# Fifty-six transposes of the identity on TensorE around the first tile of x in a hybrid decoder layer

## What is computed

```python
h = rms_norm(x, norm_w[l])
proj = jnp.einsum("btd,dc->btc", h, w_in[l])
gdn_qkv, gdn_z, gdn_b, gdn_a, moba_qkv, moba_z, gates = jnp.split(proj, SPLIT_POINTS, axis=-1)
...
merged = jax.nn.sigmoid(g_gdn) * y_gdn + jax.nn.sigmoid(g_moba) * y_moba
x = x + jnp.einsum("btd,de->bte", merged, w_o[l])
```

## Time and profile before

| | us |
|---|---|
| median of 3 runs | 1585.48 |
| lowest and highest run | 1585.01, 1586.07 |
| span of the profiled execution | 1583.4 |
| TensorE busy in it | 1559.0 |
| VectorE busy in it | 1084.3 |
| ScalarE busy in it | 797.1 |

### The profile page before, as it was taken

One profiled execution on the slowest core, in us unless ns is written; L12 is line 12 of the kernel. 1 busy time (PEld: TensorE's weight loads), 2 busy tenths in 40 slices (PEclk: granted clock), 3 DMA queues, 4 the chain that ended last, 5 costly groups with the idle time before them and its releaser, 6 DMA issues.

```text
span 1583.4 us, 20787 instructions
## 1 busy us (share of the span) xinstructions
PE 1559.0 (98%) x7767; PEld 1299.2 (82%) x7767; DVE 1084.3 (68%) x1331; ACT 797.1 (50%) x1063; POOL 191.0 (12%) x181
## 2 busy tenths in 40 slices
PE   6999999999999999999999999999999999999999
PEld 6888888888888888888888888888888887887787
DVE  6655655745646646656558778867676999978864
ACT  5434534444445445445445347556565765555542
POOL 4202001002002001011011011010101111102020
PEclk9999999999999999999999999999999999999999
DMA  8314315224234224233234338667557777878783
GB/s 270 90 32 126 81 34 149 56 62 123 54 86 115 70 57 121 60 81 98 60 86 118 119 135 252 209 171 254 131 188 191 234 234 238 231 225 176 224 183 57
DMA packets 198048, 217.04 MB, mean 137 GB/s; under 512 B 7843, under 2 KB 140198, under 8 KB 196902
## 3 DMA queue, kind: packets, MB, share of 16 engines
q1 hardware_dynamic: 177030, 162.73, 34.0%
q0 software_dynamic: 20960, 53.52, 14.7%
HBM read 191.03 MB, written 29.39 MB: 139 GB/s over the span
## 4 chain that ended last, share of the span: by engine, by line
PE 92%; DVE 3%; issue 2%; ACT 1%; DMA 1%; SPq 0%; DVEq 0%; ACTq 0%
PE bank L823 15%; PE bank L827 15%; PE bank L825 14%; PE bank L1273 11%; PE bank L1275 11%; PE bank L1277 11%; PE bank L852 2%; PE bank L928 2%; PE bank L946 1%; DVE ring_lo L2282 1%; PE bank L1023 1%; PE bank L931 1%; PE bank L857 1%; PE bank L873 1%; PE bank L874 1%
## 5 line engine op out<-in xcount | busy, mean ns | idle before, releaser
L823 PE MATMUL bank<-h_hi_r,w_hi 128*128 128x512 f32 x1008 | 408.2, 405 | 0.0
L827 PE MATMUL bank<-h_hi_r,w_raw_r 128*128 128x512 f32 x1008 | 395.0, 392 | 0.0
L825 PE MATMUL bank<-h_lo_r,w_hi 128*128 128x512 f32 x1008 | 393.4, 390 | 0.0
L2282 DVE TENSOR_TENSOR ring_lo<-operands,ring_hi 128x1024 fp32r<-128x1024 f32 x224 | 271.5, 1221 | 112.6 <-ACT ring_hi L1646 111.9
L1646 ACT ACTIVATE ring_hi<-operands 128x1024 fp32r<-128x1024 f32 x224 | 235.4, 1060 | 214.2 <-PE bank L1277 161.9
L827 PEld LDWEIGHTS bank<-h_hi_r,w_raw_r 128*128 128x128 f32 x1008 | 189.1, 188 | 41.8
L823 PEld LDWEIGHTS bank<-h_hi_r,w_hi 128*128 128x128 f32 x1008 | 189.7, 188 | 35.6
L825 PEld LDWEIGHTS bank<-h_lo_r,w_hi 128*128 128x128 f32 x1008 | 189.9, 188 | 34.7
L1273 PE MATMUL bank<-ring_hi,h_hi_r 128*128 128x512 f32 x480 | 190.2, 396 | 1.3 <-issue 1.3
L1275 PE MATMUL bank<-ring_lo,h_hi_r 128*128 128x512 f32 x480 | 188.6, 393 | 0.0
L1803 DVE TENSOR_TENSOR w_raw_r<-w_raw,w_hi 128x2048 fp32r<-128x2048 f32 x64 | 151.4, 2365 | 37.2 <-ACT w_hi L1333 36.0
(11 more groups left out here) (333 smaller groups left out, 2183.1 us busy)
## 6 DMA issues: line engine op xcount, KB each, us to landing
w_raw<-in_w_in_dram SPq DMA_DIRECT2D x64, 1024.0 KB, 6.0
operands<-in_w_in_dram SPq DMA_DIRECT2D x64, 512.0 KB, 4.6
operands<-in_w_o_dram SPq DMA_DIRECT2D x32, 512.0 KB, 5.2
operands<-in_w_in_dram POOLq DMA_DIRECT2D x16, 512.0 KB, 8.2
gates<-e_block POOLq DMA_DIRECT2D x16, 512.0 KB, 5.7
operands<-in_w_out_gdn_dram SPq DMA_DIRECT2D x16, 512.0 KB, 5.0
operands<-gates SPq DMA_DIRECT2D x16, 512.0 KB, 7.0
operands<-in_w_out_moba_dram SPq DMA_DIRECT2D x16, 512.0 KB, 5.4
```

The lines of the kernel that those rows point to most:

```text
L823: pe.matmul(PJ[slot % 2][:], w_hi[slot % 2][:, c], h_hi[:, k, :], start=(k == 0), stop=False, skip_group_check=True)
L825: pe.matmul(PJ[slot % 2][:], w_hi[slot % 2][:, c], h_lo[:, k, :], start=False, stop=False, skip_group_check=True)
L827: mm = pe.matmul(PJ[slot % 2][:], w_lo[slot][:, c], h_hi[:, k, :], start=False, stop=(k == KT - 1), skip_group_check=True)
L2282: dve.tensor_tensor(ring_lo[:, n % RINGS, :], operand(q, p, j), ring_hi[:, n % RINGS, :].bitcast(F32), ALU.subtract).then_inc(s["op_lo"], 1)
```

## The change

A helper `ready(n)` issues n transposes of `ident` by `ident` into bank A1. Forty-eight stand ahead of `x_turn(0)`, and eight between `x_turn(0)` and `x_turn(1)`. They count no semaphore. The lines behind move down by seven.

```diff
+            def ready(n):
+
+                for i in range(n):
+                    pe.transpose(A1[:, tile4(i % NT)], ident[:], ident[:])
+
+            ready(48)
             x_turn(0)
+            ready(8)
             x_turn(1)
             x_turn(2)
```

## The result

| | before | after |
|---|---|---|
| median of 21 runs, us | 1586.07 | 1588.55 |
| lowest to highest | 1584.57 to 1587.85 | 1587.42 to 1592.94 |
| span of the profiled execution | 1583.4 | 1585.9 |

The ratio is 1.0017, with a 95% interval of 1.0012 to 1.0023. The change made the kernel 2.5 us slower by the medians, 2.7 by the ratio (0.0017 x 1586). The forecast was 1585.1, the range ended at 1587.8. Of the 3.4 us between forecast and median, 0.6 lie in the kernel before, whose median over 21 runs is 1586.07 and was 1585.48 over the three known then.

What follows compares the result with a forecast made beforehand. It took TensorE, busy 98% of the span and slow-clocked until about 26.2 us, as the bound. Span 1583.4 - 0.4 = 1583.0, plus 2.08 around it, gave 1585.1 us; range 1584.0 to 1587.8.

Steps and rivals of the forecast that it cites:

- The transposes were free: Start, ahead of tile 0: the 48 fit TensorE's 8.2 us of cover if the clock rises within 6.0 us; no cost.
- ScalarE's fourth copy of hi(1): Tile 1 at the start: no longer waiting for TensorE, it starts at 19.79 instead of 20.33, gaining ScalarE 0.54 us.
- scale(3) began right behind the lo part of `w16`: VectorE, tile 3: scale(3) follows at 23.38 at once, so VectorE can use only 0.34 us of ScalarE's gain.
- VectorE decided when the products start: First-weight products: VectorE's lo part holds them, so nearly all of TensorE's 2.4 us gain turns into waiting.
- The gain of the start: First-weight products start at 30.29 instead of 30.68 us, a gain of 0.39 us.
- VectorE's work moving up: VectorE's lo part of the first weights ends at 30.15 instead of 30.49 us, 0.34 us earlier.
- the release: First-weight products: TensorE starts 0.14 us behind VectorE's end, where the kernel before showed 0.19.
- 2.08 us around the span: Whole kernel: time outside the profiled span, added to the predicted span of 1583.0 to give 1585.1 us.
- The new wait of 1.9 us ahead of the products: TensorE before the first-weight products: finished at 28.4 us, it idles 1.9 us for VectorE.
- rival 2: Start: clock rises, then falls in a gap, so tile 2 starts slow as now; 1585.4 us, chance 13%.
- Rival 1: Start: transposes do not lift the clock, so tile 0 is 2.1 us late; 1587.1 us, chance 32%.
- the last term of the costs: Fetching the extra instructions, not priced apart by the trace: taken as zero, with 0.3 us either way in the range.

Runs made afterwards that it cites:

- loop2: Second run of the changed kernel with its 48 and 8 transposes issued from two hardware loops of four each; ratio 0.9995.
- loop: Changed kernel with its 48 and 8 transposes issued from two hardware loops of four each; median 1585.67 us, ratio 0.9999 against the kernel before.
- gb: Kernel before, with the late gate load that VectorE awaits issued ahead of two operand loads instead of behind them; ratio 0.9996.
- b5: Kernel before plus 5 very small matmuls (10 pairs of weight load and matmul) ahead of tile 0; ratio 1.0000.
- b12_2: Second run of the kernel before plus 12 very small matmuls (24 pairs of weight load and matmul); ratio 0.9999.

## Why the prediction was wrong

**What held.** The transposes were free: I had the rise 5.1 us behind the first and the end at 10.7; the profile has the rise between 4.3 and 5.7 and the end at 10.9. ScalarE's fourth copy of hi(1) ran unpaced, and scale(3) began right behind the lo part of `w16`. VectorE decided when the products start: they come at 30.11, 0.05 us behind the end of L1810 and 0.23 behind the last transpose, whose pace is 0.11.

**The gain of the start came by another way.** I had 0.34 us for VectorE's work moving up and 0.05 for the release, 0.39 in all, and it was 0.57. But L1810 (L1803 before) begins at 27.78 instead of 27.85, which is 0.07 earlier, and the whole load of x came 0.09 earlier in this profile. Scale(3) did start 0.50 earlier and then took 2.25 us instead of 1.82, while GpSimd's part beside it took 1.56 instead of 3.18. Of the changed kernel, and the last row of before:

```profile
23.22 2.25 DVE L2187 SCALAR_TENSOR_TENSOR x_tiles<-x_tiles,mgt,norm_w_rows 128x1536 f32<-128x1536 f32 x1
...
23.16 1.56 POOL L681 TENSOR_SCALAR x_tiles<-x_tiles,mgt 128x512 f32<-128x512 f32 x1 [0.15 <-ACT mgt L1584]
```
```profile
23.78 3.18 POOL L681 TENSOR_SCALAR x_tiles<-x_tiles,mgt 128x512 f32<-128x512 f32 x1 [0.68 <-ACT mgt L1577]
```

The other 0.50 us are L1810 itself, 2.28 instead of 2.64 (GpSimd was through with tile 3 ahead of it this time, at 26.6 instead of 28.3; that this is the reason is not shown), and 0.14 of the release. On the release the prediction misread the rows: in the kernel before the last transpose of tile 3 started at 30.65 and the products at 30.68, so TensorE's own work came last and not VectorE, which had ended at 30.49. That the total lies near the forecast is in part luck. The sum also put 2.08 us around the span; in the changed kernel's profiled run it is 1.6 (1587.49 and 1585.9), so some 0.5 of it was that a median stood beside another execution.

**What did not come.** The new wait of 1.9 us ahead of the products: tile 2 and the beginning of `beta_alpha(0)` ran at the slow pace, so TensorE was through just when VectorE was. That is rival 2 in its first half, and loop2 shows that it doesn't happen in every execution. It cost nothing, since VectorE decides: loop, with the fall, has its products at 30.08, loop2 without it at 30.15.

**Rival 1 falls, though the time lay on its side.** Transposes of the identity alone took TensorE to the fast pace (the level of 2.4 GHz) within 6 us. The rule of the Trainium skill, "TensorE: Matmul & The Clock Gate", Part 4: PE-mode transpose, that the full clock does not engage for them, is not what this chip does with these transposes in float32; the measurement decides. By its time, 1587.1, that rival would have looked half right; its mechanism was not there. The Trainium skill's account of falls between bursts, in the same page's section on HAM oscillation, agrees with the trace of the changed kernel in that a fall came, 0.50 behind thin work and a gap of 1.65 us; in loop2 the same gap brought none.

**The step that failed** is the last term of the costs: "The extra instructions have to be fetched, which the trace does not price apart; I take zero, with 0.3 us either way in the range." In the trace it was worth up to 3.0 us, from 0.57 ahead to 2.5 behind, of which the load of the gate has some 2.2 and the load of 1436 us has 0.6. By the medians the changed kernel lies 2.0 to 2.5 us above before and the two loop kernels 0.3 to 0.5 below, so the added length is worth 2.3 to 2.9. I had looked for the price of the fetch at the place of the instructions. It was paid in the straight-line code behind the loop, by two loads on other queues that had no slack. The rows to see this were in the trace of before: single instruction packets in the list of queues, and a wait of VectorE of 1.2 us for the gates on the last-ending chain. Neither says in which direction a shift would go, but the range should have reached to the landing of that load a few microseconds later.

The start's gain is also less the change's own than it looks. The kernel gb has the start of before unchanged, and its tile 2 ran at the fast pace by itself:

```profile
20.95 1.76 PE L1203 MATMUL bank<-ident,x_tiles 128*128 128x128 f32 x12 [0.76 <-DVE h_lo_r L2188]
```

Its products started at 30.44. In two other kernels without any transpose, with a few very small matmuls at the start, they came at 30.17 (b5) and 30.10 (b12_2), as early as in the changed kernel. The moment of the rise differs from one execution to the next, and how much of the 0.57 us belongs to the change is not shown: 0.33 against gb, nothing against these two.

## What to carry to other kernels

An instruction added at the start of an unrolled program moves every later block of instructions that is fetched, and a block that falls on a load without slack can cost more than the instruction. Before believing a small gain or loss, run the same length without the work, and the same work in a hardware loop. When a time moves and the edited place does not explain it, match the traces instruction by instruction and look where the distance changes. A load that the chain waits for belongs ahead of loads that can be late; here that took most of the sensitivity away, and the next load with a waiting engine kept its own.

## What the runs showed of the hardware

- TensorE's instructions come in packets of 16384 bytes, each 256 instructions, and the packet shares the DMA engines with data: a load of 512 KB beside other loads took 8.0 to 9.3 us without a packet in it, 10.2 to 10.7 with one in its middle. Between kernels that issued it within 0.1 us of each other the price is 1.6 to 2.2 us (10.2 against 8.6, 10.7 against 8.5), up to twice the packet's own 1 us. For the load of 1436 us it is 0.7 (8.6 before, 9.3 after). Why the first is dearer is not settled.
- It happens at the start too. With 112 and 88 pairs a block came at 10.3 and 10.4 us, and tile 1 of x landed 10.2 and 10.3 us behind its issue; in the other sixteen profiles, whose first block came at 11.1 us or later, it took 8.9 to 9.7. With 112 pairs ScalarE began its square at 12.58 instead of 11.48:

```profile
12.58 1.91 ACT L1578 ACTIVATE x_square<-x_tiles 128x2048 f32<-128x2048 f32 x1 [3.72 <-DMA x_tiles<-in_x_dram]
```

- The granted clock reads 1.00 in the first microseconds, in which the pace is that of 1.2 GHz, and 0.50 only behind a rise (after 21.6 us in the changed kernel). At the start the pace must be read from start to start.
- The very small matmuls, of float32 operands, came out as two pairs of weight load and matmul each (56 in the program, 112 in the trace); a transpose is one.
